# State-space decays of a hybrid decoder step: running sums broadcast by DMA and exponentiated by ScalarE a step ahead, their TensorE products dropped

## The reference, cut to what matters

```python
a_cum = jnp.cumsum(jnp.moveaxis(a, 2, -1), axis=-1)
seg = jnp.where(tril, a_cum[..., :, None] - a_cum[..., None, :], -jnp.inf)
Lmat = jnp.exp(seg)                                   # decay from token s to token l, per head
CB = jnp.einsum('bclgn,bcsgn->bcgls', Cc, Bc)
y_diag = jnp.einsum('bcgls,bcgels,bcsgep->bclgep', CB, Lmat, xdt)
...
y_off = jnp.einsum('bclgn,bcgepn,bcgel->bclgep', Cc, h_prev, jnp.exp(a_cum))
```

## Time and profile before

| | |
|---|---|
| three timed runs | 1470.52, 1475.45, 1480.02 us (median 1475.45) |
| the profiled execution's own time | 1470.6 us |
| its span from first to last instruction | 1469.1 us |
| mean granted TensorE clock | 0.991 |
| state-space stage | about 484 to 953 us of the span |

### The profile page before, as it was taken

One profiled execution on the slowest core, in us unless ns is written; L12 is line 12 of the kernel. 1 busy time (PEld: TensorE's weight loads), 2 busy tenths in 40 slices (PEclk: granted clock), 3 DMA queues, 4 the chain that ended last, 5 costly groups with the idle time before them and its releaser, 6 DMA issues. The chain is left out here.

```text
span 1469.1 us, 27147 instructions
## 1 busy us (share of the span) xinstructions
PE 1399.0 (95%) x10581; PEld 1302.6 (89%) x10581; DVE 818.8 (56%) x1194; ACT 663.0 (45%) x1118; POOL 222.5 (15%) x398
## 2 busy tenths in 40 slices
PE   4999999989989999999999999999999999999997
PEld 4998777888879998888888887899999999999997
DVE  3454455777843466777687676874444444442221
ACT  4565445766731355574464574533333333231211
POOL 3002133000022213323223213112000000000010
PEclk9999999999999999999999999999999999999999
DMA  3225565112256424334434426362222222323331
GB/s 118 73 72 164 181 214 160 55 60 68 68 111 200 107 85 126 108 89 129 116 96 130 115 80 192 107 192 73 87 75 83 86 86 75 87 77 102 95 96 48
DMA packets 201109, 157.35 MB, mean 107 GB/s; under 512 B 13672, under 2 KB 187216, under 8 KB 200959
## 3 DMA queue, kind: packets, MB, share of 16 engines
q1 hardware_dynamic: 175394, 97.93, 23.0%
q0 software_dynamic: 25232, 57.70, 13.5%
q10 hardware_dynamic: 384, 0.37, 0.1%
HBM read 132.04 MB, written 23.91 MB: 106 GB/s over the span
## 5 line engine op out<-in xcount | busy, mean ns | idle before, releaser
L450 PE MATMUL tile_banks<-x_hi,w_hi 128*128 128x288 f32 (+1 forms) x1808 | 529.7, 308 | 18.0 <-ACT gate_out L1739 14.0
L451 PE MATMUL tile_banks<-x_lo,w_hi 128*128 128x288 f32 (+1 forms) x1808 | 507.6, 296 | 0.0
L454 PE MATMUL tile_banks<-x_hi,w_lo 128*128 128x288 f32 (+1 forms) x1808 | 386.5, 295 | 0.0
L450 PEld LDWEIGHTS tile_banks<-x_hi,w_hi 128*128 128x128 f32 (+1 forms) x1808 | 341.3, 189 | 33.6 <-issue 25.6
L451 PEld LDWEIGHTS tile_banks<-x_lo,w_hi 128*128 128x128 f32 (+1 forms) x1808 | 341.7, 189 | 5.4 <-issue 3.6
L424 DVE TENSOR_TENSOR w_lo<-w_raw,w_hi 128x1024 fp32r<-128x1024 f32 (+2 forms) x169 | 206.9, 1224 | 173.4 <-ACT w_hi L418 172.2
L454 PEld LDWEIGHTS tile_banks<-x_hi,w_lo 128*128 128x128 f32 (+1 forms) x1808 | 291.0, 188 | 0.4
L418 ACT ACTIVATE w_hi<-w_raw 128x1024 fp32r<-128x1024 f32 (+2 forms) x169 | 175.7, 1039 | 103.2 <-PE tile_banks L454 101.8
L451 PE MATMUL tile_banks<-f_lo,w_hi 128*128 128x288 f32 x352 | 98.1, 295 | 0.0
L450 PE MATMUL tile_banks<-f_hi,w_hi 128*128 128x288 f32 x352 | 97.9, 294 | 0.0
L454 PE MATMUL tile_banks<-f_hi,w_lo 128*128 128x288 f32 x352 | 73.9, 291 | 0.0
(11 more groups left out here) (381 smaller groups left out, 2461.1 us busy)
## 6 DMA issues: line engine op xcount, KB each, us to landing
w_raw<-in_w_in SPq DMA_DIRECT2D x68, 512.0 KB, 3.6
w_raw<-in_w_gate SPq DMA_DIRECT2D x22, 512.0 KB, 3.6
w_raw<-in_w_up SPq DMA_DIRECT2D x22, 512.0 KB, 3.6
k_page<-in_cache_k SPq DMA_DIRECT2D x64, 128.0 KB, 2.4
v_page<-in_cache_v POOLq DMA_DIRECT2D x64, 128.0 KB, 2.9
old<-in_state_ssm POOLq DMA_DIRECT2D x32, 256.0 KB, 3.6
out_ssm_sample<-old POOLq DMA_DIRECT2D x32, 256.0 KB, 3.0
w_raw<-in_w_pb SPq DMA_DIRECT2D x16, 512.0 KB, 3.3
```

The costliest lines, as they stand in the source:

```text
L450: nc.tensor.matmul(out, wh, xh[:, HALVES[h]], start=start and k == 0, stop=False, skip_group_check=onto)
L451: nc.tensor.matmul(out, wh, xl[:, HALVES[h]], start=False, stop=False, skip_group_check=onto)
L454: mm = nc.tensor.matmul(out, wl, xh[:, HALVES[h]], start=False, stop=stop and k == last, skip_group_check=onto)
```

## The change

The six-block matrix in DRAM becomes a plain table of sums, 5 chunks x 32 heads x 128. POOL fetches for each step the rows of the group's 8 heads and writes them to all 128 partitions (512 KB in place of 256 KB). ScalarE subtracts: `Relu(a_cum[s] - a_cum[l])` per head, 8 instructions of 128 x 128 with the per-token column `sum_tok` as bias, in place; then one `Exp` with scale -1 for all 8 heads. For l < s the exponent is cut off at 0 and the mask that `cb_m` already holds zeroes the entry. `e_t` comes from the same rows ahead of the Relu, in two instructions of 64 partitions, and has two buffers. The segment products, `picks`, `past` and `a_signed` go. The exponentials of step c + 1 (and `e_t` of step c + 2) are made at the end of step c; `xend` and the product with `cb_m` (`prepare`) for step c + 1 too. For c > 0 `new_outputs` moves from behind slice 8 of `one` (or slice 4 of `two`) to directly behind `old_and_state`. The sums are made straight from `dt_tok`, ahead of `decays`.

```diff
@@ POOL
+                eng.dma_start(sum_rows[:, st % 2, :, 0:m], sums_dram[c, g * HG:(g + 1) * HG, 0:m].partition_broadcast(P)).then_inc(sem(f"sums_in{st % 2}"), 16)
-                eng.dma_start(sum_rows[0:2 * NH, st % 2], sums_matrix(c)).then_inc(sem(f"sums_in{st % 2}"), 16)
@@ TensorE, loop over c
-                    segments(g, c)
                     gemm(one, range(0, 4))
                     gemm(None if one else two, range(0, 3))
                     old_and_state(g, c)
+                    if c:
+                        new_outputs(g, c)
                     gemm(one, range(4, 8))
                     gemm(None if one else two, range(3, 4))
-                    new_outputs(g, c)
+                    if c == 0:
+                        new_outputs(g, c)
@@ ScalarE
+            def bounded_sums(st):
...
+                rows = sum_rows[0:m, st % 2, :, 0:m]
+                eng.wait_ge(sem(f"sums_in{st % 2}"), 16 * (st // 2 + 1))
+                wait_after_read(eng, ("sums", 1))
+                if c:
+                    eng.wait_ge(sem("e_made"), g * NC + c)
+                for h in range(HG):
+                    ins = eng.activation(rows[:, h, :], rows[:, h, :], ACT.Relu, scale=-1.0, bias=sum_tok[0:m, c, g * HG + h:g * HG + h + 1])
+                ins.then_inc(sem("sums_bounded"), 1)
+            def decays(st):
...
+                if st:
+                    wait_full(eng, ("y_new", (st - 1) // 5, (st - 1) % 5))
...
+                eng.activation(decay[0:m, :, 0:m], sum_rows[0:m, st % 2, :, 0:m], ACT.Exp, scale=-1.0).then_inc(sem("decay_raw"), 1)
+            def e_rows(g, c):
...
+                for e in range(2):
+                    rows = slice(e * HD, (e + 1) * HD)
+                    ins = eng.activation(e_t[rows, n % 2, :, 0:m], sum_rows[rows, st % 2].rearrange("p (j e) l -> p j e l", e=2)[:, :, e, 0:m], ACT.Exp)
+                ins.then_inc(sem("e_made"), 1)
@@ ScalarE, loop over c
-                    segments(g, c)
                     if c == 0:
                         xend_hi(g)
+                    bounded_sums(g * 5 + c + 1)
                     if one:
                         slot(one)
                     if two:
                         next_hi(two)
...
+                    decays(g * 5 + c + 1)
+                    if c + 2 <= NC:
+                        e_rows(g, c + 2)
                     if two:
                         empty(two)
@@ VectorE, loop over c
-                    prepare(g, c)
+                    if c == 0:
+                        prepare(g, c)
...
+                    prepare(g, c + 1)
                     if two:
                         empty(two)
```

More of the change, by code:

```diff
@@ L293, in build @@
         cb_m = sb("cb_m", [P, 5, P], F32, ssd)
-        sum_rows = sb("sum_rows", [P, 2, HG, P], F32R, ssd)
-        sums = sb("sums", [P, T], F32R, ssd)
-        picks = sb("picks", [P, T + P + HD], F32R, ssd)
+        sum_rows = sb("sum_rows", [P, 2, HG, P], F32, ssd)
+        sums = sb("sums", [NH, T], F32, ssd)
+        sum_tok = sb("sum_tok", [P, 5, NH], F32, ssd)
         decay = sb("decay", [P, HG, P], F32, ssd)
-        e_t = sb("e_t", [P, PG, P], F32, ssd)
+        e_t = sb("e_t", [P, 2, PG, P], F32, ssd)
         state = sb("state", [P, HG * HD], F32, ssd)
@@ L309, in build @@
         seq_decay = sb("seq_decay", [P, NH // 2, NB], F32, ssd)
-        a_signed = decay[:, 0:5, :].rearrange("p c (k h) -> p c k h", k=4)
         a_seq = conv_out[0:TS].rearrange("p c k -> p (c k)")[:, P:P + NH * NB].rearrange("p (h b) -> p h b", b=NB)
-        state_out = e_t
+        state_out = e_t[:, 0]
         conv_rows = [xdt[0:27, j].rearrange("p h d -> p (h d)") for j in range(5)] + [xend[0:27].rearrange("p h d -> p (h d)")]
@@ L359, in build @@
         FIRST_USES = len(keys)
-        keys += [("decays", 0), ("sums", 0), ("sums", 1)]
+        keys += [("sums", 0), ("sums", 1), ("decays", 0)]
         for g in range(NG):
@@ L1247, in _ @@
                 mm.then_inc(tile_done, 1)
+            key = ("sums", 1)
+            for c, t0, m in token_tiles():
+                pe.matmul(spare(key)[0:m, TS + NH * c:TS + NH * (c + 1)], (upto if c < NC else upto_b)[0:m, 0:m], dt_tok[0:m, c, NH:2 * NH],
+                          start=c == 0, stop=True, skip_group_check=True)
+            for c, t0, m in token_tiles():
+                key = ("sums", c // NC)
+                mm = pe.matmul(spare(key)[0:NH, t0 % TP:t0 % TP + m], dt_tok[0:m, c, NH:2 * NH], (upto if c < NC else upto_b)[0:m, 0:m],
+                               start=c == 0, stop=True, skip_group_check=True)
+                if c >= NC - 1:
+                    mm.then_inc(bank_full[use[key][0]], 1)
             key = ("decays", 0)
@@ L1961, in _ @@
                 by_token(g)
+                decays(g * 5)
+                e_rows(g, 1)
                 plan = ssd_plan(g)
@@ L2427, in prepare @@
                     make_xend(g, c)
-                for q in range(2):
-                    wait_after_read(eng, ("seg", g, c, q))
+                eng.wait_ge(sem("decay_raw"), g * 5 + c + 1)
                 wait_after_read(eng, ("cb", g) if c < NC else ("sample_bc", g))
```

160 lines of the change are left out of this document (35 added, 125 removed).

## The result

The changed kernel takes 1492.25 us (median of four runs, 1490.2 to 1498.7) beside 1475.3 us for the kernel before on the same chip. The ratio is 1.0124, with a 95% interval of 1.0098 to 1.0149: **slower by 1.2%**, where I predicted 1458 us and gave "slower" 0.13. The profiled run took 1490.99 us with a span of 1489.5.

The account below looks back on a forecast made before the run. The prediction took TensorE, busy 1399.0 of 1469.1 us, to bound the kernel. Its terms, 3.4 - 4.8 + 10.2 + 11.2 - 3 = 17 us, came off the 1475.45 us median to give 1458 us, range 1440 to 1477.

Parts of the forecast that it names:

- start of the stage: Before the state-space stage's first tiles: 2.2 us from an earlier start and 1.2 us from the clock, 3.4 us gained.
- steps 0: First step of each of four groups: Relus and `e_t` delay `w_lo` or the old states' copy, 4.8 us lost together.
- double steps: Step 1 of group 0 gains 1.8 us, six in groups 1 and 2 gain 1.4 each: 10.2 us gained.
- single steps: Steps 2 to 4 of group 0, 4 of groups 1 and 2, 1 to 4 of group 3: 11.2 us gained.
- transfers: Fetch of the sums, now 512 KB, and the old states' round: 1.5 us lost each, 3 us together.
- price on TensorE: Segment products leaving TensorE: 7.6 us a group, 30.2 us over four groups, the most the steps can give.
- ScalarE's Relus: Eight Relus a step on ScalarE: pitch 0.16 us, about 1.4 us together; other end pitch 0.28, 2.2 us.
- rival 2: ScalarE's turn costs more, Relus at 0.28 pitch and idle times pulling the clock down: 7 us gain, 1468; chance 0.2.
- rival 3: Broadcast of the sums lands late and stalls single steps: at 15 us landing, net 18 slower, 1493; chance 0.13.

Follow-up runs that it names:

- e1: Changed kernel with VectorE emptying a pb tile's two banks before the next step's decays are multiplied (`prepare`): 1480.07 us, ratio 1.0045.
- e4: Changed kernel with one Relu a step in place of eight, so the decays are other numbers: 1485.62 us, ratio 1.0079.
- e6: e3 plus a third buffer for the sequences' states, one load issued at the head of a step: 1472.06 us, ratio 0.9964.
- e10: e7 with `new_outputs` put back in its old place behind the fourth to seventh slices: 1455.4 us, ratio 0.9882.
- f2: e3 with `new_outputs` put back in its old place: ratio 0.9963.
- b1: Kernel before, with the product of the picks and the sums dropped and only the mask multiplied: 1472.38 us, ratio 0.9970.
- e7: e3 plus the edits of both e5 and e6, first pb bank early and third states buffer: 1461.23 us, ratio 0.9903.
- e3: Changed kernel with two orders changed, pb banks emptied before `prepare` and `w_hi` made before the Relus: 1475.95 us, ratio 1.0013.
- e5: e3 with VectorE emptying a pb tile's first bank between a step's two sequences: 1465.28 us, ratio 0.9930.
- f3: The same kernel as e10, timed a second time: 1460.91 us, ratio 0.9897.

## Why the prediction was wrong

**The terms side by side.** Cut at the same matmuls in both traces, the start of the stage gained 3.2 us (3.4 predicted); the four steps 0 lost 13.2 (4.8); step 1 of group 0 and the six double steps of groups 1 and 2 lost 9.0 (10.2 **gained**); the single steps gained 2.1 (11.2, less 3 for the transfers); what lies between the groups and behind the last one lost 2.2 (nothing predicted). That is 19.1 us, the account's sum.

**Start of the stage: right.** 3.4 us predicted. From the last attention tile to the first of the stage it is 5.1 us, 7.5 before, and the 1.2 us of half clock behind it are gone: 3.6. The clock's part was luck: e1, e4, e6, e10 and f2 have the same order there and no idle time over 0.3 us, and in each the granted clock was 0.50 for 3.4 us at 490 us all the same.

**The price on TensorE: right.** 28.8 us of work by the account, 30.2 predicted.

**ScalarE's Relus: mis-sized.** A pitch of 0.29 us, 2.44 for eight, where I took 0.16 and 1.4 from the full-width copies. The row of the 32-partition copies (0.28), my other end, was the right one. In step 0 of group 0 this made 4.13 us of waiting from 2.9, and the 3.4 us of half clock behind it, which I had only in rival 2, came on top: the step is 7.2 us longer, not 2.1. Those of groups 1 and 2 are 1.8 us longer each, not 0.7: `w_lo` waits of 2.09 where they were 0.97, `old_t` behind the Relus, 0.98 and 1.74, and a stretch of half clock in group 1. That of group 3 is 2.4 us longer, not 1.3.

**Double steps: this step failed.** I had +10.2 us. Read from `y_seq`'s last transpose to the next, step 1 of groups 1 and 2 went from 20.2 and 20.1 to 19.0 and 18.9, about as predicted. Steps 2 and 3 went from 20.1 each to 22.6 and 23.3 (group 1), 24.2 and 23.5 (group 2). I had followed the chain behind the end of `one` through the earlier trace rows and found 0.7 us of room; I had not asked what VectorE owes at the end of a step. `pb` tiles use both pairs of banks, and `prepare` in front of their emptying is in the diff. The listed order of VectorE shows it too. e1 measures this oversight at 12 us, in double and single steps together.

**The cover: the deeper error.** I counted each removed product as time won unless a chain in the row showed otherwise, on the ground that a double step had TensorE busy for all its 20.17 us. A busy TensorE at the head of a step only says that the wait there is shorter than the product. In b1, where nothing was added or moved, 5.2 of 9.3 us turned into gaps. In f2, with the three orders that cost most put back, the work is 29.2 us less and the gaps are 31.8 - 12.1 = 19.7 us more. That is up to two thirds of the work; f2 still has the Relus and the exponentials at the end of the step, and no run parts their share from the cover.

**Single steps: this failed too.** Steps 2 to 4 of group 0 gained 1.1 us (3.6 predicted; the terms given for them add up to 1.56 + 0.26 + 0.7 = 2.5 only), steps 1 to 4 of group 3 1.8 us (4.8), and the steps 4 of groups 1 and 2 lost 0.8 where I had kept 2.8. Step 1 of group 3 lost 2.5, with 2.77 us of waiting for `pb_sum`; in step 4 of group 0 a wait of 1.36 us for `w_lo` took the place of the 1.43 us of products.

**The moved `new_outputs`** had no price in my sum; it cost 2 to 4 us of waits.

**Transfers and rival 3: wrong.** Landing takes 4.9 us, nobody waits for it, and the 1.5 us that I took for late sums were not needed; the kernel is slower by another mechanism. By the Trainium skill (DMA: Bandwidth & Descriptors, Measured (HBM→SBUF, 128 partitions, SWDGE, issued from GpSimd)) the estimate was 3 us for 512 KB and no loss; the row has 4.9 from issue to landing, which is more than the transfer alone that the page times, and the loss is indeed nought. Rival 2, late turns of ScalarE and half clock, had a part of the loss and 10 us for it; the kernel came out 34 us behind the forecast, and the half clock alone is 11.9. The largest sum of waits, 19.7 us for `pb_sum`, is in no rival.

## What to carry to other kernels

Before you credit a removed instruction on the bounding engine, ask what would be ready if it were not there: follow the other engines' queues up to that point, and look for the end that lies just inside the instruction you take away. It ended 0.42 us inside here. When work is moved ahead "into idle time", read what stands behind it in its queue; a PSUM bank waiting to be emptied is worth more than a product made a step early. And test an edit on both kernels: the early emptying was worth nothing before and 10.7 us after (7.7 us of gaps), so a change that brings nothing may still be half of one that does.

## What the hardware showed that I had not expected

**The same matmuls at two rates with the full clock.** In the windows of 1240 to 1320 us at the top, nothing but feed-forward tiles runs, TensorE is busy for all 80 us and the clock is 1.00 in both, but 611 matmuls start in one and 597 in the other: 131 and 134 ns from start to start. The best kernel (e10) is at the fast rate there:

```profile
1240.00:1320.00 80.00, 80.00 (x610) 80.00 (x609) 32.95 (x36) 22.98 (x26) 0.00 (x0) 1.00 0.28 82
```

and e7, which differs from it in one order long before, at the slow one:

```profile
1240.00:1320.00 80.00, 80.00 (x597) 80.00 (x596) 31.84 (x35) 21.98 (x26) 0.00 (x0) 1.00 0.29 84
```

A trace can change from one to the other halfway. Over the last 3000 tile matmuls this makes 396.7 us (before), 400.8 (after) and 404.0 (e1, e3, e4), while e5 has 397.7 and b1, on the old code, 400.8. It follows no edit that I made: e10 and f3 are the same kernel, with 397.5 and 401.0. What sets it stays open; it is of the size of the spread between runs of one kernel (some 10 us), and it is a reason not to read a difference of 5 us from one profile.

**Idle time costs twice, but not always.** The granted clock went to 0.50, the lower level of 1.2 GHz, for 3.4 us or twice that, mostly behind idle times such as the 4.13 us in step 0, and each such stretch cost 1.7 or 3.4 us. In e1, e4, e6, e10 and f2 it did so at 490 us too, where TensorE had been busy with the small products of the sums and decays. The changed kernel has eight stretches, 15.3 us in all; e3 with waits of 2.4 us at most has 5.1, e5 with fewer gaps than e3 has 12.0. I cannot say from these runs which gap brings it.

**The short in-place Relu** of 128x128 with a bias per partition runs at 0.29 us from start to start, the plain copy from PSUM of the same size at 0.16.

**A broadcast read is no slower than the fetch that it replaced.** 512 KB to 128 partitions that all read the same 4 KB land in 4.9 us on GpSimd's queue; 256 KB of separate rows took 5.5 there. On SyncE's queue a weight chunk of 512 KB took 3.9 in the same stage of the changed kernel, so what the broadcast itself costs is not shown.
